# Depthwise convolution of two mixer layers: from VectorE, spread over the layer, to GpSimd, as one stream

## The reference, cut to what matters

```
def conformer_branch(a, b, z, w_dw, b_dw, ln_g, ln_b):
    u = a * jax.nn.sigmoid(b)
    c = (depthwise_conv(u, w_dw) + b_dw.astype(u.dtype)).astype(F32)   # 31 taps
    mu = jnp.mean(c, axis=-1, keepdims=True)
    var = jnp.mean(jnp.square(c - mu), axis=-1, keepdims=True)
    n = (c - mu) * lax.rsqrt(var + EPS) * ln_g.astype(F32) + ln_b.astype(F32)
    return jax.nn.silu(n).astype(a.dtype) * jax.nn.silu(z)
...
for n, yb in enumerate((y_hg, y_cf, y_sc, y_at, y_mem)):
    term = jax.nn.sigmoid(h @ w_gate[l, n]) * (yb @ w_branch[l, n])
    merged = term if merged is None else merged + term
x = x + rmsnorm(merged @ w_out[l], norm_post[l])
```

## Time and profile before

| | |
|---|---|
| median of 3 runs (lowest, highest) | 1691.52 us (1689.47, 1692.62) |
| the profiled execution's own time | 1692.9 us |
| its span in the profile | 1689.6 us |
| mean granted clock of PE | 0.952 |
| busy PE / DVE / ACT / POOL | 93% / 77% / 19% / 1% |
| HBM traffic | 147 GB/s over the span |

### The profile page before, as it was taken

The page is one execution under the profiler, slowest core; times in us unless marked ns, Lnnn a source line. Parts: engine busy times, 40 slices in busy tenths (PEclk is TensorE's granted clock), DMA queues, the critical chain, the costliest instruction groups (busy, mean ns, idle before and its releaser), DMA issues.

```text
span 1689.6 us, 26299 instructions
## 1 busy us (share of the span) xinstructions
PE 1573.2 (93%) x11298; PEld 1449.1 (86%) x11298; DVE 1306.7 (77%) x1576; ACT 328.8 (19%) x669; POOL 23.2 (1%) x49
## 2 busy tenths in 40 slices
PE   6899999979999999989988899999989789999997
PEld 6888989968989899889857899999889578999996
DVE  6698888678888896766747877878866777787877
ACT  3422410122333201120241200000011911000000
POOL 0000000000000000010000000000000000000000
PEclk9999999999999999989768899999989989999999
DMA  7435635433445345245302445555545033555562
GB/s 229 140 100 174 235 104 188 162 112 125 150 150 175 125 150 179 83 159 155 120 1 87 138 150 191 183 182 188 180 154 193 3 125 125 175 180 194 175 199 75
DMA packets 205330, 249.87 MB, mean 148 GB/s; under 512 B 5098, under 2 KB 190570, under 8 KB 205216
## 3 DMA queue, kind: packets, MB, share of 16 engines
q1 hardware_dynamic: 199328, 226.60, 41.7%
q0 software_dynamic: 5072, 18.73, 3.2%
q10 hardware_dynamic: 816, 2.87, 0.5%
HBM read 246.09 MB, written 2.10 MB: 147 GB/s over the span
## 4 chain that ended last, share of the span: by engine, by line
PE 70%; DVE 22%; ACT 5%; issue 1%; DMA 1%; DVEq 0%; ACTq 0%
PE bank L382 49%; PE bank L793 10%; DVE wL L1389 5%; DVE wH L1387 3%; PE bank L575 2%; DVE proj L1562 1%; DVE work L1581 1%; PE bank L693 1%; PE bank L728 1%; PE bank L411 1%; DVE MT L1751 1%; DVE L L1747 1%; PE bank L707 1%; DVE work L1616 1%; ACT proj L1361 1%
## 5 line engine op out<-in xcount | busy, mean ns | idle before, releaser
L382 PE MATMUL bank<-hH,wH 128*128 128x256 f32 x2384 | 690.0, 289 | 19.8 <-DVE wL L1389 13.0
L382 PE MATMUL bank<-hL,wH 128*128 128x256 f32 x2384 | 679.7, 285 | 0.0
L382 PE MATMUL bank<-hH,wL 128*128 128x256 f32 x2384 | 679.4, 285 | 0.0
L382 PEld LDWEIGHTS bank<-hH,wH 128*128 128x128 f32 x2384 | 462.9, 194 | 31.3 <-DVE wL L1389 22.4
L1389 DVE TENSOR_TENSOR wL<-ring,wH 128x2048 fp32r<-128x2048 f32 x210 | 479.5, 2283 | 7.2
L382 PEld LDWEIGHTS bank<-hL,wH 128*128 128x128 f32 x2384 | 463.0, 194 | 2.0
L382 PEld LDWEIGHTS bank<-hH,wL 128*128 128x128 f32 x2384 | 462.6, 194 | 0.0
L1387 DVE CAST wH<-ring 128x2048 fp32r<-128x2048 f32 x210 | 256.9, 1223 | 46.9 <-PE bank L382 25.4
L793 PE MATMUL bank<-wH,hidR 128*128 128x512 f32 x512 | 170.3, 404 | 1.3 <-DVE hidR L1409 1.3
L382 PE MATMUL bank<-wH,hH 128*128 128x256 f32 (+1 forms) x400 | 117.0, 292 | 7.7 <-DVE hL L1409 7.7
L793 PEld LDWEIGHTS bank<-wH,hidR 128*128 128x128 f32 x512 | 98.9, 193 | 25.4 <-issue 2.6
(11 more groups left out here) (369 smaller groups left out, 1585.4 us busy)
## 6 DMA issues: line engine op xcount, KB each, us to landing
ring<-in_w_gate SPq DMA_DIRECT2D x40, 1024.0 KB, 5.3
ring<-in_w_in SPq DMA_DIRECT2D x34, 1024.0 KB, 5.5
ring<-in_moe_w_gate SPq DMA_DIRECT2D x32, 1024.0 KB, 5.3
ring<-in_moe_w_up SPq DMA_DIRECT2D x32, 1024.0 KB, 5.2
ring<-in_moe_w_down SPq DMA_DIRECT2D x32, 1024.0 KB, 4.9
ring<-in_sb_w_in SPq DMA_DIRECT2D x12, 1024.0 KB, 5.1
ring<-in_ab_w_in SPq DMA_DIRECT2D x11, 1024.0 KB, 5.2
ring<-in_w_out SPq DMA_DIRECT2D x8, 1024.0 KB, 5.3
```

What stands on the lines that cost most here:

```text
L382: last = mm(ps[:, m * CW:m * CW + (width if token_major else S)], a, b, start=k == 0 and i == 0, stop=k == KT - 1 and i == 2)
```

## The change

The taps leave DVE's stream. POOL runs all 124 instructions of a layer in one go: for each tap a product of the shifted `convs` with the weight, broadcast along the row, into a new tile `ptap`, and an addition of `ptap` to `convc` (for the first tap of a tile, of the bias to `ptap`). Each waits for the one before through `pool_done`. In layer 0 the stream stands after the three small loads and ahead of the wait for the `rel` tiles and L924. In layer 1 it stands after the gain's load and ahead of the loads of `w_branch`. It starts when DVE has written `convs` (`emptied_at(("ca", l))`). PE's wait for `conv_ready` is as before. DVE gets a wait for the previous layer's `conv_ready` before it writes `convs` in layer 1. A wait for `consts_made` on POOL at the start is new too.

```
+        ptap_place = nc.sbuf_tensor("ptap", [P, S], F32)
...
+            def taps(l):
+
+                eng.wait_ge(*emptied_at(("ca", l)))
+                for j, k in TAPS:
+                    c = convc[:, j * S:(j + 1) * S]
+                    u = convs[:, j, k:k + S]
+                    w = pcol(("dw", l), j, k)
+                    if k == 0:
+                        g.tensor_tensor(ptap, u, w.to_broadcast([P, S]), ALU.mult).then_inc(pool_done, 1)
+                        eng.wait_ge(pool_done, own(pool_done))
+                        ins = g.tensor_tensor(c, ptap, pcol(("dwb", l), j).to_broadcast([P, S]), ALU.add)
+                    else:
+                        g.tensor_tensor(ptap, u, w.to_broadcast([P, S]), ALU.mult).then_inc(pool_done, 1)
+                        eng.wait_ge(pool_done, own(pool_done))
+                        ins = g.tensor_tensor(c, c, ptap, ALU.add)
+                    done = conv_ready if (j, k) == TAPS[-1] else pool_done
+                    ins.then_inc(done, 1)
+                    eng.wait_ge(done, own(done))
...
+            eng.wait_ge(consts_made, own(consts_made))
...
+            taps(0)
             for h in range(AT_HEADS):
                 eng.wait_ge(*emptied_at(("rel", h)))
             eng.dma_start(rel_d.ap().rearrange("h p n -> p h n"), relwide).then_inc(rel_stored, 16)
...
                 eng.dma_start(gain[:, 0, :], io["norm_post"][l].partition_broadcast(P)).then_inc(gain_loaded, 16)
+                if l:
+                    taps(l)
                 for b, n in enumerate(ORDER):
...
+                        if l:
+                            eng.wait_ge(conv_ready, l)
                         tt(convs[:, :, CONF_K // 2:CONF_K // 2 + S], tiles3(ps[:, :]), tiles3(convc),
...
-                def taps(step):
-
-                    first = sum(TAP_PLAN[:step])
-                    for j, k in TAPS[first:first + TAP_PLAN[step]]:
-                        c = convc[:, j * S:(j + 1) * S]
-                        u = convs[:, j, k:k + S]
-                        w = pcol(("dw", l), j, k)
-                        if k == 0:
-                            ins = ts(c, u, w, pcol(("dwb", l), j), ALU.mult, ALU.add)
-                        else:
-                            ins = stt(c, u, w, c, ALU.mult, ALU.add)
-                        done = conv_ready if (j, k) == TAPS[-1] else ve_done
-                        ins.then_inc(done, 1)
-                        eng.wait_ge(done, own(done))
...
-                        taps(i - 1)
...
-                    taps(len(LEVELS) - 1 + i)
...
-                    if g < MEAN_AT:
-                        taps(len(LEVELS) - 1 + ASTEPS + g)
```

More of the change, by code:

```diff
@@ L125, in build @@
         identR = sb("identR", [n_exp, n_exp], F32R)
+        ptap_place = nc.sbuf_tensor("ptap", [P, S], F32)
+        ptap = ptap_place.__enter__()[:, :]
+        ptap_place.__exit__(None, None, None)
         comR = sb("comR", [n_exp, 2, S], F32R)
@@ L322, in build @@
         MEAN_AT, VAR_AT, CONF_AT = 7, 10, 12
-        TAP_PLAN = [1] * (len(LEVELS) - 1) + [2] * ASTEPS
-        TAP_PLAN += [-(-(len(TAPS) - sum(TAP_PLAN)) // MEAN_AT)] * MEAN_AT
         head_slot = lambda h: h // 2 + 2 * (h % 2)
```

## The result

The changed kernel takes 1734.22 us (median of 4, 1732.34 to 1737.11), the kernel before 1691.28 beside it: ratio 1.0256, 95% interval 1.0238 to 1.0274. It is slower by 43 us, in the direction and range forecast, 15 us under the 1749 predicted. Its profiled execution has a span of 1735.0 us, 45.4 over the one of before.

The account below looks back on a forecast made before the run. PE bounds it (busy 93%), DVE next. Per layer: 41 us of DVE waits, less 3.9 of taps and 4 absorbed, 33; less 4 regained, +29. Two layers' 58 on 1692.9 give 1751, median 1749; range 1677 to 1795.

Parts of the forecast that it names:

- Gain of a lighter DVE, 12 us: Levels and attention: without taps on DVE, PE wins 6 of the 7.8 us it lacks a layer, 12 for two.
- Price of a POOL instruction, 0.61 us: POOL's stream: 0.61 us an instruction, bounds 0.31 and 0.83; 0.66 a period, 82 us a layer undisturbed.
- A: Levels: DVE's contending instructions and POOL's exclude each other and alternate; 1749 us, own range 1710 to 1795, chance 0.45.
- 0.55 us held for each of the 74: Levels of layer 0: each of 74 contending DVE instructions waits 0.55 us for one POOL instruction, 41 us in all.
- 4 us of a layer's wait absorbed by the small gaps: Levels: PE's and DVE's small gaps absorb 4 of 37 us, so the levels end 33 us later.
- The stream ends with the levels, L924 isn't held up: Layer 0: all 124 POOL instructions fit by the levels' end, so the store L924 behind them isn't held up further.
- PE's clock costs nothing extra: Whole kernel: PE's clock adds no time, since PE would be waiting anyway.
- 4 us back a layer for the lighter DVE: After the stream: DVE is lighter by 26 us, of which PE can use 4 us, making +29 a layer.
- B: DVE keeps the port and POOL starves, running only when DVE doesn't contend; +36, 1727 us, chance 0.18.
- C: DVE and POOL don't disturb each other; stream over at 149 us, -12 us, 1680, chance 0.20.
- D: Only DVE's fast modes meet POOL: 11 casts in the levels wait 0.55 us each; no change, 1692, chance 0.10.
- E: No contention, but POOL slower than the upper bound, say 1.2 us; stream 50 us late, 1722, chance 0.07.

Follow-up runs that it names:

- e2: The changed kernel without the convolution: convc cleared by one POOL memset a layer, no taps on DVE or POOL; 1675.05 us, ratio 0.9917.
- e9: The changed kernel with store and bias loads on ACT, POOL's stream started after the levels, and the mean two gate products later; 1723.74 us, ratio 1.0208.
- e3: The changed kernel with each layer's 124 POOL instructions replaced by memsets of 128x512 and the convolution left out; 1681.47 us, ratio 0.9964.
- e4: The kernel before, taps kept on DVE, plus POOL's stream into scratch that nobody reads, store and bias loads on ACT; 1744.56 us, ratio 1.0321.
- e1: The changed kernel with the rel store and the two bias loads issued by ACT instead of POOL; 1720.55 us, ratio 1.0177.
- e6: As e1, but each POOL instruction works on 128 columns in place of 256; 1695.38 us, ratio 1.0024.
- e5: As e1, but each tap's product and the bias are a POOL tensor_scalar with one weight per partition; 1715.54 us, ratio 1.0145.

## Why the prediction was right

- *Gain of a lighter DVE, 12 us:* 9.4 in block one (e2).
- *Price of a POOL instruction, 0.61 us:* 0.609 for the product, as taken, and 0.722 for the addition, 0.11 more; the bounds 0.31 and 0.83 held. Undisturbed, at the start of e9's stream, a product and an addition take 1.49 us with the gaps, 0.75 each where 0.66 was taken; that is 10 us more for the 124.
- *The two exclude each other and alternate:* as predicted, the mechanism of A. e3 and e4 show it from both sides: reading is what holds, and it costs the time with nothing else changed. The Trainium skill (SBUF — State Buffer, Who interferes with whom) says that a DVE instruction with two SBUF inputs contends with GpSimd's reads and not with one that only writes. With that the traces agree: DVE's products take 0.43 us beside the memsets of e3 and 0.75 to 0.87 beside the stream.
- *0.55 us held for each of the 74:* this is the term that was mis-sized. It was 0.34 (25.1 us over 74). The count of 74 was right; 74 x 0.34 = 25.1, less 3.9 of taps gone, is 21, and the levels grew by 19.0 and 21.9 where 33 were forecast. The profiled duration of a POOL instruction was taken for its hold; DVE waits for only about half of it. The "whole instruction" of the Trainium skill (SBUF — State Buffer, Who interferes with whom) doesn't hold in that sense: in the timeline the 2.29 us subtraction is held 0.29 us by a product of 0.61.
- *4 us of a layer's wait absorbed by the small gaps:* too much. DVE's idle time in the levels of layer 0 fell by 2.0 us, from 13.1 to 11.1, and in layer 1 the levels grew by 21.9, with nothing absorbed.
- *The stream ends with the levels, L924 isn't held up:* wrong, by 8.5 us. It ended at 204 us, 20 after the levels. The forecast had both near 165 + 33 = 198. The stream came 6 us later than that; the levels ended 14 earlier, since DVE was held less. The store also took 8.4 us in place of 4.3. e1 gives these back.
- *PE's clock costs nothing extra:* this fits the levels, where DVE sets the pace, but not attention. There the granted clock was 0.90 in the changed kernel, 1.00 before and 0.95 in e1, and 3.2 of the 9.6 us that e1 gives back are PE's busy time.
- *4 us back a layer for the lighter DVE:* 4.3 in layer 1; in layer 0 only 1.1, as e1's attention shows (72.3 against 73.4).
- The sum with the measured terms, against block one's end: 19.0 + 8.5 - 0.1 in layer 0 and 21.9 - 4.3 in layer 1 make 45.0 of 45.2.
- That 58 forecast and 45 measured lie so near is luck in part, because the errors cancel. The smaller hold takes 31 us off the forecast for the two layers. The gaps that absorbed less put 6.5 back, and layer 0 after its levels, 8.5 lost where 4 were to be won, 12.5: 46 in all.
- Rivals: B is excluded by DVE's durations, C by e4, D by the products' 0.8 us, E since POOL's own time is 0.61 to 0.72.

Left open: why the hold falls to a third with half of the columns (e6), and which part of e5's gain is a shorter hold. POOL's shortest durations are 0.67 us in the mean with a hold of 0.34, and 0.42 with one of 0.11, so that some 0.3 us of each would not hold DVE. Two points don't show such a rule, and e5's product, at 0.92 us, held DVE's subtractions and casts less, which speaks against it.

## What to carry to other kernels

POOL isn't free beside a busy VectorE. In this kernel a POOL instruction that reads SBUF took a turn from every VectorE instruction that reads two SBUF inputs or is a cast or `tensor_scalar` in a fast form: 0.34 us for 256 columns, about 0.11 for 128, and two such instructions replaced one tap of 0.485. Count the VectorE instructions that will meet the stream, and multiply by a hold that was measured, not by what the POOL instruction lasts in the profile; and ask in which stages VectorE is part of a chain of turns between engines, for there the sum is paid. A long stream on a queue that also issues DMAs belongs behind them.

## What the runs showed of the hardware that was not expected

- A `tensor_scalar` with a weight per partition takes POOL 0.92 us for 128x256, longer than the 0.61 of a `tensor_tensor` with a broadcast column (e5, e1), and disturbs VectorE less.
- A POOL memset of 128x512 (0.52 us) delays VectorE's cast from 1.23 to 1.61 us and leaves two-input instructions alone.
- The second block, with the same code in every kernel, lasts 955.7 to 963.5 us from the end of block one to the end of the span in the profiled executions. The ten runs of e3 fall into 1680 to 1682 us (granted clock 0.951 to 0.955) and 1690 to 1691 (0.949 to 0.950), four of them in the second. Of the 7.0 us between e2 and the kernel before, 5 are PE's busy time for the same 6276 matmuls (902.6 against 907.6 us). Differences of 8 us and more between medians can come from there. The marks by stage lie ahead of the second block; how much block one itself varies isn't shown, since each kernel has one profile.
